# One unsplit weight unit in 24 in place of two, and a reordered passage from the router to the experts

## What is computed

```python
g_sel = jnp.argmax(g_logits + b_group, axis=-1)                     # 1 of 4 groups
_, e_local = lax.top_k(e_logits + e_bias, TOP_K)                    # 2 of its 8 experts
...
def ffn(args):                                                      # per expert, D 2048, FF 512
    xb, e = args
    return (jax.nn.silu(xb @ w1[e]) * (xb @ w3[e])) @ w2[e]
```

## Time and profile before

| what | value |
|---|---|
| median of 3 runs | 2145.46 us (2145.35 to 2146.33) |
| profiled execution, its own time | 2144.49 us |
| its span in the trace | 2142.7 us |
| PE busy | 2056.4 us (96%) |
| DVE busy | 1593.0 us (74%) |
| ACT busy | 1272.4 us (59%) |
| loads by SP's queue | 593.81 MB |

### The profile page before, as it was taken

How to read it: one execution, slowest core, us unless ns; L and a number is a source line. 1 busy time by engine, 2 the same in 40 slices (tenths; PEclk the granted TensorE clock), 3 DMA queues, 4 the chain that set the end, 5 groups by cost and what they waited for, 6 DMA issues and landing times.

```text
span 2142.7 us, 29970 instructions
## 1 busy us (share of the span) xinstructions
PE 2056.4 (96%) x11454; PEld 1742.3 (81%) x11454; DVE 1593.0 (74%) x1412; ACT 1272.4 (59%) x1060; POOL 106.0 (5%) x77
## 2 busy tenths in 40 slices
PE   8999999999999999999999999999999999999992
PEld 8998888899999998887887778777777778777861
DVE  7646654453636375445669999999999999999997
ACT  5435663333332323333347888888888888888872
POOL 1000000000000000001000000000000000000001
PEclk9999999999999999999999999999999999999996
DMA  6545335655454544557758999999999999999993
GB/s 214 156 139 159 118 119 185 209 178 176 143 172 156 158 156 156 187 188 242 237 217 316 413 421 421 421 422 418 422 420 418 415 423 420 417 417 419 418 414 149
DMA packets 164608, 602.50 MB, mean 281 GB/s; under 512 B 20321, under 2 KB 28657, under 8 KB 113425
## 3 DMA queue, kind: packets, MB, share of 16 engines
q1 hardware_dynamic: 160816, 593.81, 72.9%
q0 software_dynamic: 3712, 7.59, 1.2%
HBM read 595.05 MB, written 18.89 MB: 287 GB/s over the span
## 4 chain that ended last, share of the span: by engine, by line
PE 66%; DVE 16%; issue 8%; DMA 7%; ACT 3%; DVEq 0%; POOLq 0%; POOL 0%; SPq 0%; ACTq 0%
PE ps L1851 19%; PE ps L1832 15%; DVE wl L702 10%; DMA raw<-in_w_dram 7%; PE ps L1024 6%; PE ps L1025 5%; PE ps L2202 4%; PE ps L1021 4%; ACT wh L562 2%; PE ps L1046 2%; PE ps L1957 2%; PE ps L1937 2%; PE ps L994 1%; PE ps L1924 1%; DVE yall L858 1%
## 5 line engine op out<-in xcount | busy, mean ns | idle before, releaser
L702 DVE TENSOR_TENSOR wl<-raw,wh 128x2048 fp32r<-128x2048 f32 x351 | 789.8, 2289 | 37.6 <-ACT wh L562 36.3
L562 ACT ACTIVATE wh<-raw 128x2048 fp32r<-128x2048 f32 x351 | 668.9, 1915 | 137.6 <-DMA raw<-in_w_dram 77.1
L1422 DVE TENSOR_TENSOR wl<-raw,wh 128x2048 fp32r<-128x2048 f32 (+1 forms) x168 | 379.9, 2264 | 284.4 <-ACT wh L1224 284.3
L1224 ACT ACTIVATE wh<-raw 128x2048 fp32r<-128x2048 f32 (+1 forms) x168 | 318.1, 1896 | 444.7 <-DMA raw<-in_w_in_dram 271.8
L1024 PE MATMUL ps<-wh,xg 128*128 128x512 f32 x896 | 372.1, 415 | 22.1 <-DVE wl L702 21.7
L1025 PE MATMUL ps<-wl,xg 128*128 128x512 f32 x896 | 350.8, 392 | 0.0
L1832 PE MATMUL ps<-hth,wh 128*128 128x272 f32 (+1 forms) x896 | 259.7, 290 | 3.2 <-DVE wl L1422 1.8
L1832 PE MATMUL ps<-htl,wh 128*128 128x272 f32 (+1 forms) x896 | 255.8, 285 | 0.0
L1832 PE MATMUL ps<-hth,wl 128*128 128x272 f32 (+1 forms) x896 | 255.6, 285 | 0.0
L1024 PEld LDWEIGHTS ps<-wh,xg 128*128 128x128 f32 x896 | 168.6, 188 | 74.1 <-DVE wl L702 27.8
L1024 PE MATMUL ps<-wh,hx 128*128 128x512 f32 x508 | 202.1, 398 | 3.5 <-issue 2.4
(11 more groups left out here) (351 smaller groups left out, 3065.5 us busy)
## 6 DMA issues: line engine op xcount, KB each, us to landing
raw<-in_w_dram SPq DMA_DIRECT2D x384, 1024.0 KB, 10.2
raw<-in_w_in_dram SPq DMA_DIRECT2D x103, 1024.0 KB, 5.1
raw<-in_w_pa_dram SPq DMA_DIRECT2D x16, 1024.0 KB, 5.0
raw<-in_w_pb_dram SPq DMA_DIRECT2D x16, 1024.0 KB, 5.0
raw<-in_w_out_dram SPq DMA_DIRECT2D x16, 1024.0 KB, 5.2
raw<-in_w_ukv_dram SPq DMA_DIRECT2D x8, 1024.0 KB, 5.3
yrow<-yscr SPq DMA_DIRECT2D x4, 1024.0 KB, 7.8
raw<-in_w_uq_dram SPq DMA_DIRECT2D x8, 384.0 KB, 3.5
```

The costliest lines, as they stand in the source:

```text
L562: nc.scalar.activation(wh2[:, x % HELD, :], raw2[:, slot2(x), :], ACT.Copy).then_inc(s_wh2, 1)
L702: nc.vector.tensor_tensor(wl2[:, slot2(x), :], raw2[:, slot2(x), :], wh2[:, x % HELD, :].bitcast(F32), ALU.subtract).then_inc(s_wl2, 1)
L1224: nc.scalar.activation(wh[:, n % RING1, 0:c], raw1[:, n % RING1, 0:c], ACT.Copy).then_inc(s_wh, 1)
L1422: nc.vector.tensor_tensor(wl[:, n % RING1, 0:c], raw1[:, n % RING1, 0:c], wh[:, n % RING1, 0:c].bitcast(F32), ALU.subtract).then_inc(s_wl, 1)
```

## The change

It has two parts. In each pair unit 10 is no longer unsplit: ScalarE rounds it, VectorE writes its remainder, TensorE multiplies it in two halves; unit 22 stays unsplit. And the passage is ordered differently: the unused matmuls go from 24 + 5 x 3 to 12 + 21 x 1, the router's maximum moves behind the stream's remainder and is not waited for, unit 4 is rounded before the gathered banks are copied, the second token tile's gathers of banks 2 to 6 go behind unit 0 and the gather of bank 7 behind unit 1, the next pair's `pg` goes behind the remainder of unit 5, and in the first pair the `hidden` comes one unit earlier, with ScalarE's sigmoid behind the rounding.

```diff
-        XR = (10, 22)
+        XR = (22,)
@@ scalar_experts: hi, pair, start
-                if isinstance(turn, int) and 24 * turn + x < HELD:
+                if isinstance(turn, int) and 24 * turn + x <= HELD:
                     act.wait_ge(s_wused, N_UNITS)
+                    if x + HELD != HELD or not early:
+                        hi(turn, x + HELD)
                     if k == 14 and early:
                         sigmoid(2 * turn)
-                    hi(turn, x + HELD)
-            hi(0, 2)
-            hi(0, 3)
+            for x in (2, 3, 4):
+                hi(0, x)
@@ vector_experts: first_max, ranks, pair
-                routed.append(own.count)
+            routed.extend(range(begun + 1, own.count))
-            own.after(nc.vector.scalar_tensor_tensor(r2[:, :, :], pr, 1.0, asg[:, :, :], ALU.add, ALU.mult))
-            nc.vector.tensor_reduce(rs[:, 18:19], r2[:, :, :].rearrange("p t e -> p (t e)"), AXX, ALU.max).then_inc(s_mxr, 1)
             for t in range(TT):
                 stream_rest(t)
+            own.after(nc.vector.scalar_tensor_tensor(r2[:, :, :], rk_[:, :, 0:E], 1.0, asg[:, :, :], ALU.add, ALU.mult))
+            nc.vector.tensor_reduce(rs[:, 18:19], r2[:, :, :].rearrange("p t e -> p (t e)"), AXX, ALU.max).then_inc(s_mxr, 1)
-                    if k == 0 and first:
+                    if k == 2 and first:
                         gather_matrix(turn + 1, 2 * p + 2)
-                    if k == 14 and early:
+                    if k == 13 and early:
                         hidden(2 * turn, 0, turn)
@@ tensor_experts
-            keep_warm(24)
+            keep_warm(12)
             for step_ in routed:
                 pe.wait_ge(s_dve, step_)
-                keep_warm(3)
+                keep_warm(1)
                     if early and k == 0:
+                        for q in range(2, 7):
+                            first_gather(q, 1, (1,))
+                    if early and k == 1:
                         pe.wait_ge(s_xg, 1)
                         for h in range(2):
                             first_gather(7, h, (0, 1))
-            keep_warm(3, 0)
+            keep_warm(4, 0)
             pe.wait_ge(s_pg, 1)
-            pe.wait_ge(s_mxr, 1)
             pe.wait_ge(s_xh1, TT)
-                keep_warm(4, 0)
+                keep_warm(8 if t else 3, 0)
                 pe.wait_ge(s_xl1, t + 1)
-                for q in range(7):
+                for q in range(2 if t else 7):
                     first_gather(q, 1, (t,))
```

More of the change, by code:

```diff
@@ L728, in vector_experts @@
             routed.append(own.count)
+            begun = own.count
             for t in range(TT):
```

## The result

The changed kernel took 2151.19 us (median of 11 runs, 2150.41 to 2154.92), the kernel before 2145.40 us beside it (11 runs, 2143.92 to 2147.78): 1.0026 times as long, with a 95% interval of 1.0018 to 1.0033. The profiled execution took 2150.58 us (span 2148.8), 6.09 us more than the 2144.49 of before. The forecast was 2151.8 us and +6.3 for the profiled execution. Beside the later runs the median of the kernel before lies between 2145.99 and 2146.95 us, so a distance of 1 us between medians that were not measured side by side says little.

A forecast was written before the change was run, and what follows sets the result against it. Loads bound late pairs at 60.76 us; the change passes the bound to the loop of ScalarE, VectorE and TensorE at 61.03. Terms 5.6 + 1.7 - 1.0 = +6.3 us, forecast 2151.8 us, range 2145.5 to 2155.0.

The forecast's parts named there:

- What bounds the kernel: Expert stage: loads set late pairs at 60.76 us; the engines' own loop needs 60.07; the slower counts.
- The price of unit 10: VectorE, unit 8 to unit 14: added remainder of 2.20 us less 1.24 idle, so 0.96 more; loop 61.03 us.
- The idle behind unit 22: VectorE's idle of 0.51 us behind unsplit unit 22 in each pair stays.
- the prediction's own signs: Profile signs of being wrong: pairs of 60.7 to 60.8, idle beyond 0.5 us ahead of units 2 or 14, first pair off 1181.4.
- a higher loop: Rival, expert loop: a quarter or more of the 1.24 us returns as another wait; 61.3 or more, from 2155.5 us; chance 0.08.
- 14 pairs: Unit 20 of the first pair to unit 20 of the fifteenth: 14 x 61.03 = 854.42 us, +5.6 us.
- The passage: Ahead of the expert stage: unit 0 earlier, gain lost by unit 5; first pair's unit 20 comes 1.7 us later.
- The end: Unit 20 of the fifteenth pair to the last hidden product, at the loop's pace: -1.0 us.
- Loads that keep the pace: Rival, expert pairs: loop stays under 60.76 us, pairs cost as before; 2143.8 to 2147.2 us; chance 0.17.
- VectorE landing whole: Rival, expert stage: 16 remainders of 2.20 us add 35 us; 2180.7 us; chance 0.03.
- a bound on TensorE: Rival, expert stage: 16 x 1.66 = 26.6 us gained; 2118.9 us; chance 0.01.
- The clock: TensorE ahead of unit 0: about 1 us more waiting from fewer unused matmuls; nothing set down for the clock.

The follow-up runs named there:

- the half loads: Only half of unit 22 loaded, that half multiplied twice: in the kernel before 2137.66 us (ratio 0.9956), in the changed kernel 2150.70 us (1.0021).
- runs 5 to 8: Half of unit 22 loaded, kernel before: 0.9956; same, changed kernel: 1.0021; changed kernel with unit 10 unsplit, 22 split: 1.0055; changed kernel with both split: 1.0110.
- run 4: The changed kernel with nine unused matmuls on TensorE ahead of the first pair's first `mix`: 2150.78 us, ratio 1.0018.
- run 7: The changed kernel with the other unit kept, unit 10 unsplit and unit 22 split: 2157.29 us, ratio 1.0055.

## Why the prediction was right

**What bounds the kernel.** Right, and shown by the half loads: 60.76 a pair falls to 60.09 in the kernel before, the 60.07 read from its second and third pair, and the changed kernel's 61.02 does not move.

**The price of unit 10.** Right. The stretch from unit 8 to unit 14 was put at 14.93 us; it is 1468.60 + 2.20 - 1455.88 = 14.92. Of 2.20 us VectorE had 1.24 free. The Trainium skill's rule (Perfetto Trace Analysis, section "Identifying the Most-Contended Engine") would still name VectorE, now busy 686.43 of 700 us. The rows agree with that occupancy, and show that an added 2.20 us cost 0.93 at unit 10 and 1.28 at unit 22.

**The idle behind unit 22.** Right in its sum, not in its parts. It was said to stay at 0.51; it is 0.81, and a smaller one of 0.24 ahead of unit 23, which no term named, is gone. From unit 20 to unit 2 it is 13.97 us as before (13.98): TensorE's unsplit product sets the end of that stretch, whatever VectorE does inside it. By the prediction's own signs an idle beyond 0.5 us ahead of unit 2 was to mean a higher loop; the idle came and the higher loop did not, because the smaller idle had gone. That the missing term did no harm was luck: it showed only where unit 22 itself was split, and there the sum was 0.33 us too high.

**14 pairs.** 854.23 us against the forecast 854.42.

**The passage.** Unit 0 at 1127.29 (forecast 1127.1), unit 5's remainder at 1137.79 (1137.6), unit 20 at 1181.39 (1181.4). That the copies of the banks take back what unit 0 gains was right: unit 0 starts 1.52 us earlier than before, unit 5's remainder only 0.2. With two unsplit units the passage is worth nothing that the medians can tell.

**The end.** -0.99 us against -1.0.

**The rivals.** Loads that keep the pace, VectorE landing whole and a bound on TensorE are excluded by pairs of 61.0 us and by runs 5 to 8. A higher loop didn't come.

**The clock.** Wrong. Nothing was set down for it, because TensorE had kept 1.00 with 5.55 of 8 us busy. It fell all the same in the first pair. In the profiled execution it cost nothing, as run 4 and the rows of VectorE show, so the sum came out although this term was put at nothing for a reason that did not hold; in another execution it cost 0.5 us. Of the unsplit unit it had been said only that the 1.66 us which TensorE saves buy nothing. That unit had also filled TensorE's time ahead of the first `mix`.

## What to carry to other kernels

Where loads, an engine's loop and another engine all look full, read the pace of the loop in a stretch in which nobody waits for loads, and the pace of the loads where they do; an edit that lifts the lower of the two costs only what it rises above the higher. An added operation costs its length less the idle that the same edit removes, and that has to be summed over the whole stretch to the next point which another engine sets, the small idles too. A wait that is taken away at one unit may come back at the next if both stand behind the same long operation, so follow the second waiter before counting the gain.

## What the hardware did that was not expected

The granted clock of TensorE fell to its lower level, 0.50 or 1.2 of 2.4 GHz, in the first pair of the expert stage, for some 7 us. Split matmuls then started 0.43 us apart (1161.28, 1161.71) instead of 0.23. The wait of 2.31 us and windows of 2.54 and 1.16 busy us of 3 preceded it; in the kernel before the windows from 1159 to 1165 held 2.12 and 1.44 busy us of 3, and it stayed at 1.00.

In the run with unit 22 split (run 7) the same happened once in the loop, for 3.4 us, behind a wait of 1.88 us. These are its windows of 1 us:

```profile
1643.00:1644.00 1.00, 0.07 (x1) 0.07 (x1) 1.00 (x2) 1.00 (x1) 1.00 (x1) 1.00 0.98 410
1644.00:1645.00 1.00, 1.00 (x3) 0.82 (x4) 1.00 (x1) 0.48 (x1) 0.64 (x1) 0.52 1.01 418
```

That pair took 62.88 us in place of 61.34. VectorE stood idle for 1.31 us in it, ahead of a remainder whose rounding waited for TensorE. In the run with no unsplit unit (run 8) the clock fell in the first pair of the expert stage and six times behind it, and from unit 20 to unit 20 on VectorE no pair is over 62.29 us, whether the clock fell in it or not. So a fall of a few microseconds was free where VectorE found its next units rounded, and that pair of run 7 was 1.54 us longer with one.
